# Moving the operand arena and the tile of block rests by 64 bytes in a hybrid two-block kernel

## The chip, the cores and the metric

The kernel runs on one core of a Trainium2 chip. The metric is the device time of one execution in microseconds, taken as the median of several executions. One execution was also recorded by the hardware profiler, and all rows shown here come from that record.

## The reference

The program computes two stacks of two layers each over a sequence of 512 tokens with 1024 features, all in float32. The first stack has in each layer a SwiGLU feed-forward, a mixer made of four parts (top-k sparse attention, gated linear attention, a causal convolution, and low-rank attention with rotary positions), and a second feed-forward. The second stack has a dilated-attention layer with a state-space part, then a layer with a gated linear recurrence, each followed by a feed-forward. Cut to what carries nearly all of the work:

```python
def rmsnorm(x, g):
    y = x32 * lax.rsqrt(jnp.mean(x32 * x32, axis=-1, keepdims=True) + EPS)
    return (y * g.astype(jnp.float32)).astype(x.dtype)

def swiglu(x, w_gate, w_up, w_down):            # [512,1024] x [1024,2816], twice; [512,2816] x [2816,1024]
    return (jax.nn.silu(x @ w_gate) * (x @ w_up)) @ w_down

def hybrid_layer(x, ...):                       # two of these
    x = x + 0.5 * swiglu(rmsnorm(x, ffn1_norm), ffn1_gate, ffn1_up, ffn1_down)
    z = rmsnorm(x, mix_norm) @ w_in
    ...                                         # four mixers on parts of z
    x = x + y @ w_out
    x = x + 0.5 * swiglu(rmsnorm(x, ffn2_norm), ffn2_gate, ffn2_up, ffn2_down)
    return x

def second_block(x, ...):                       # two layers
    mix = even_mixer(hn, ...) or odd_mixer(hn, ...)
    x = x + rms_norm(mix, norm_mix_post[layer])
    ff = swiglu_2(rms_norm(x, norm_ffn_pre[layer]), ffn_w_gate[layer], ffn_w_up[layer], ffn_w_down[layer])
    x = x + rms_norm(ff, norm_ffn_post[layer])
```

## The kernel before

Activations lie transposed: features on the 128 partitions, tokens along a row. A large product is made of matmuls with a stationary operand of 128x128 weights, which a weight load puts into the array, and a moving operand of 128 partitions by 512 or 256 tokens, which then streams through it. The next matmul's weight load runs while the present matmul streams, so TensorE reads two places of SBUF at once: the weights of the next matmul and the tokens of the present one.

Each float32 product is computed from split operands. A value is rounded to the type fp32r (the "hi" part) and the rest is kept beside it (the "lo" part). ScalarE writes the hi parts, VectorE the rests, and TensorE adds three products for each pair of tiles: weights hi by tokens hi, weights lo by tokens hi, weights hi by tokens lo. In `split_product` these are the lines L969, L970 and L971, always with 512 tokens. The tiles are `w_hi` (in `scratch`) and `w_lo` (in `wring`) for the weights, and for the tokens `f_hi`/`f_lo` (input of the six feed-forwards), `g_hi`/`g_lo` (their hidden values) and `z_hi` (input of the first stack's mixer projections), all in `arena`; `xn_hi` (input of the output projections and of the odd layer's projection) in `att_diag`; and `xn_lo` (the rests that go with `xn_hi` and `z_hi`) in `xn`.

The middle part of each of the six feed-forwards (`pe_ffn7`) computes its gate and up products in halves, by a scheme of seven block products instead of eight. Seven blocks j = 0 to 6 of weights, 128 partitions by 512 values each, are sums or differences of raw weight blocks. Each block takes 12 matmuls of 256 tokens: four pieces k, each with L1080 (block hi by `t_hi`), L1082 (block rest by `t_hi`) and L1083 (block hi by `t_lo`). The block rests lie in `p_lo_tile`, which shares its place with the raw sums `p_raw` in `att_diag`. `t_lo` lies in `arena`; `t_hi` lies in `xn` for blocks 0 to 3 (`t_hi_early`) and in `arena` for blocks 4 to 6 (`t_hi_late`). One group of seven blocks is one "kind" (gate or up) of one pair of hidden tiles. There are 9 pairs of 2 kinds in each of 6 feed-forwards, so 108 groups.

```python
            nc.tensor.matmul(ps, w_hi[:, slot, t, 0:M], hi, start=start, stop=False)
            nc.tensor.matmul(ps, w_lo[:, slot, t, 0:M], hi, start=False, stop=False)
            return nc.tensor.matmul(ps, w_hi[:, slot, t, 0:M], lo, start=False, stop=stop)
...
                            nc.tensor.matmul(ps, hi[:, k, :], t_hi(j)[:, k, :], start=(not again and k == 0), stop=False,
                                             skip_group_check=again)
                            nc.tensor.matmul(ps, lo[:, k, :], t_hi(j)[:, k, :], start=False, stop=False, skip_group_check=again)
                            mm = nc.tensor.matmul(ps, hi[:, k, :], t_lo[:, j, k, :], start=False, stop=(k == KH - 1),
                                                  skip_group_check=again)
```

The order of the work is written out by hand for each engine, with semaphores between them. The addresses within a partition are given by the order of allocation. `sb_aligned` puts a gap ahead of a tile so that it begins at a multiple of 512 bytes. The tiles `x`, `xn`, `wring`, `scratch`, `bias`, `arena` and `att_diag` all begin so. Every piece inside them is 512, 1024 or 2048 bytes long, with one exception: in `p_lo_tile` and `p_raw` the blocks are 2048 + 64 bytes apart (`BLK + GAP`, GAP being 16 words), so block j begins 64 x j bytes behind a multiple of 512.

Of the kernel before, what the change touches and what calls it, by code (L numbers as in the profile page):

```python
# [9 lines left out]
F32 = mybir.dt.float32  # L10
# [6 lines left out]
P = 128  # L17
SEQ = 512
TB = SEQ // P
# [11 lines left out]
B_HEADS, B_KEY, B_VAL, B_CHUNK, B_RANK = 4, 32, 64, 64, 16  # L31
# [194 lines left out]
HALF = SEQ // 2  # L226
KH = KD // 2
BLK = KH * P
GAP = 16
SCALED, FIRST_S3 = (1, 2, 5, 6), (3, 4)  # L230
SCALED_SUMS = 5 + GROUPS - 1
SUMS = KD + 4 + 3 * GROUPS
# [118 lines left out]
def program(nc, I, out):  # L351
    ctx = ExitStack()
    with ctx:
        at = {}

        def sb(name, shape, dt=F32):
            at[name] = -(-nc.sbuf_base // 32) * 32
            return ctx.enter_context(nc.sbuf_tensor(name, shape, dt))

        def over(name, shape, base, skip=0):  # L360

            return nc.alloc_sbuf_tensor_at(name, shape, F32R, offset=at[base] + skip)
# [4 lines left out]

        ALIGN = 512

        def sb_aligned(name, shape):  # L370
            gap = -(-(-nc.sbuf_base // 32) * 32) % ALIGN
            if gap:
                ctx.enter_context(nc.sbuf_tensor(f"gap_before_{name}", [P, gap // 4], F32))
            return sb(name, shape)

        x = sb_aligned("x", [P, KD, SEQ])
        xn = sb_aligned("xn", [P, KD, SEQ])
        y = xn
        wring = sb_aligned("wring", [P, 2, KD, 256])
        scratch = sb_aligned("scratch", [P, 11, SEQ])  # L380
        bias = sb_aligned("bias", [P, A_HEADS, SEQ])
        arena = sb_aligned("arena", [P, 46, SEQ])
        att_diag = sb_aligned("att_diag", [P, TB, B_HEADS, P])
        sb("block_gaps", [P, 8 * GAP])
        xn_more = sb("xn_more", [P, 2, SEQ])
        hpad = sb("hpad", [P, 2, TAPS - 1 + SEQ])
        b_mn, b_la = xn_more[:, 0, :], xn_more[:, 1, :]
# [29 lines left out]
        t_lo = over("t_lo", [P, 7, KH, HALF], "arena", 22 * SEQ * 4)  # L417
        t_hi_early = over("t_hi_early", [P, 4, KH, HALF], "xn")
        t_hi_late = over("t_hi_late", [P, 3, KH, HALF], "arena", 36 * SEQ * 4)
        p_lo_tile = over("p_lo_tile", [P, 8, BLK + GAP], "att_diag")[:, :, 0:BLK]  # L420
        p_raw = nc.alloc_sbuf_tensor_at("p_raw", [P, 8, BLK + GAP], F32, offset=at["att_diag"])[:, :, 0:BLK]
        g_lo = over("g_lo", [P, NF, SEQ], "arena")
        g_hi = over("g_hi", [P, NF, SEQ], "arena", 22 * SEQ * 4)
        gup = sb("gup", [B_RANK, P])
# [2963 lines left out]
```

## Time and profile before

| what | value |
|---|---|
| median of the runs | 3308.72 us (3306.56 to 3310.53, 3 runs) |
| the profiled execution, its own time | 3307.32 us |
| its span, first to last instruction | 3305.2 us |
| TensorE matmuls busy | 3196.7 us (97%), 18272 matmuls |
| weight loads busy | 2682.5 us (81%), beside the matmuls |
| VectorE busy | 2249.8 us (68%) |
| ScalarE busy | 1536.8 us (46%) |
| mean granted clock of TensorE | 0.989 |

The profiled execution took 2.1 us more than its span, and 1.4 us less than the median of the runs. A matmul's busy time in the profile includes its way through the array and overlaps with that of the next matmul, so what a matmul costs in a stream is the step from its start to the next one's start, and not its mean duration.

### The profile page before, as it was taken

What the parts mean: (1) busy time and instruction counts of PE and PEld (TensorE: products, weight loads), DVE (VectorE), ACT (ScalarE), POOL (GpSimd) and SP (SyncE); (2) the same over time, 40 slices, a digit from 0 to 9 for tenths busy, and PEclk for the clock granted to TensorE, in tenths of its full rate; (3) what the DMA queues carried; (4) which work ended last, traced back from release to release, by engine and by line L of the source; (5) the groups of instructions that cost most, each with busy time, mean ns of one, the idle gap of its engine ahead of it and who ended that gap; (6) DMA issues with size and microseconds to landing.
All of it is one profiled execution on the core that took longest, in us unless ns stands there. A gap on an engine that the chain in (4) does not pass through costs nothing.

```text
span 3305.2 us, 51513 instructions
## 1 busy us (share of the span) xinstructions
PE 3196.7 (97%) x18272; PEld 2682.5 (81%) x18272; DVE 2249.8 (68%) x3675; ACT 1536.8 (46%) x2795; POOL 241.7 (7%) x153
## 2 busy tenths in 40 slices
PE   7999999999999999999899999999899999999998
PEld 5998775779988899876578998565689986779986
DVE  5884489649854986388938873844398736679853
ACT  4553345445543554344535553213355524555543
POOL 0000002100000000000200000401000003110000
PEclk9999999899999999999999999999999999999999
DMA  4332331023323333332013332341133323223332
GB/s 140 107 102 100 85 83 53 1 81 100 113 96 95 100 104 97 100 83 78 1 52 100 104 101 90 97 95 37 52 90 102 102 96 95 72 78 106 102 102 76
DMA packets 420154, 286.41 MB, mean 87 GB/s; under 512 B 57416, under 2 KB 395180, under 8 KB 419884
## 3 DMA queue, kind: packets, MB, share of 16 engines
q1 hardware_dynamic: 419200, 283.62, 28.9%
q8 instruction: 77, 1.26, 0.2%
q10 hardware_dynamic: 828, 1.13, 0.1%
q14 instruction: 49, 0.40, 0.0%
HBM read 280.24 MB, written 4.47 MB: 86 GB/s over the span
## 4 chain that ended last, share of the span: by engine, by line
PE 79%; DVE 15%; ACT 3%; issue 3%; DMA 0%; POOL 0%; ACTq 0%; DVEq 0%; SPq 0%; POOLq 0%
PE bank L969 12%; PE bank L971 12%; PE bank L970 12%; PE bank L1080 10%; PE bank L1082 10%; PE bank L1083 10%; DVE t_lo L2388 1%; PE bank L964 1%; PE bank L1340 1%; PE bank L1339 1%; PE bank L1358 1%; DVE p_lo_tile L2361 1%; DVE w_lo L2347 1%; DVE arena L2419 1%; PE bank L1454 1%
## 5 line engine op out<-in xcount | busy, mean ns | idle before, releaser
L1083 PE MATMUL bank<-t_lo,w_hi 128*128 128x256 f32 x3024 | 851.3, 282 | 0.0
L2347 DVE TENSOR_TENSOR w_lo<-wring,w_hi 128x1024 fp32r<-128x1024 f32 x262 | 331.9, 1269 | 576.9 <-ACT w_hi L1707 576.5
L1707 ACT ACTIVATE w_hi<-wring 128x1024 fp32r<-128x1024 f32 x274 | 288.4, 1059 | 652.6 <-DMA wring<-in_ffn_down 278.5
L1083 PEld LDWEIGHTS bank<-t_lo,w_hi 128*128 128x128 f32 x3024 | 571.3, 189 | 0.0
L1082 PE MATMUL bank<-t_hi_early,p_lo_tile 128*128 128x256 f32 x1728 | 486.7, 282 | 0.0
L1080 PE MATMUL bank<-t_hi_early,w_hi 128*128 128x256 f32 x1728 | 485.6, 281 | 0.0
L971 PE MATMUL bank<-g_lo,w_hi 128*128 (+1 forms) x1056 | 410.9, 389 | 0.0
L970 PE MATMUL bank<-g_hi,w_lo 128*128 (+1 forms) x1056 | 410.8, 389 | 0.0
L969 PE MATMUL bank<-g_hi,w_hi 128*128 (+1 forms) x1056 | 410.8, 389 | 0.0
L1080 PE MATMUL bank<-t_hi_late,w_hi 128*128 128x256 f32 x1296 | 366.2, 283 | 9.8 <-ACT scratch L1795 8.9
L1082 PE MATMUL bank<-t_hi_late,p_lo_tile 128*128 128x256 f32 x1296 | 365.6, 282 | 0.0
L1719 ACT ACTIVATE w_hi<-p_raw 128x512 fp32r<-128x512 f32 x432 | 267.4, 631 | 199.4 <-DVE p_raw L2380 121.6
L2361 DVE TENSOR_TENSOR p_lo_tile<-p_raw,w_hi 128x512 fp32r<-128x512 f32 x432 | 287.9, 687 | 66.6 <-ACT w_hi L1719 56.7
L1082 PEld LDWEIGHTS bank<-t_hi_early,p_lo_tile 128*128 128x128 f32 x1728 | 328.2, 190 | 0.2
L1080 PEld LDWEIGHTS bank<-t_hi_early,w_hi 128*128 128x128 f32 x1728 | 326.9, 189 | 0.2
L1795 ACT ACTIVATE scratch<-bank 128x256 f32<-128x256 f32 x432 | 165.8, 384 | 274.8 <-PE bank L1083 267.6
L971 PE MATMUL bank<-xn_lo,w_hi 128*128 128x512 f32 (+1 forms) x680 | 266.9, 393 | 0.0
L2361 DVE TENSOR_TENSOR p_lo_tile<-wring,w_hi 128x512 fp32r<-128x512 f32 x324 | 222.7, 687 | 59.9 <-ACT w_hi L1719 56.8
L1080 PEld LDWEIGHTS bank<-t_hi_late,w_hi 128*128 128x128 f32 x1296 | 245.0, 189 | 12.0 <-issue 11.9
L1082 PEld LDWEIGHTS bank<-t_hi_late,p_lo_tile 128*128 128x128 f32 x1296 | 246.8, 190 | 0.0
L971 PEld LDWEIGHTS bank<-g_lo,w_hi 128*128 128x128 f32 x1056 | 198.2, 188 | 41.1
L970 PEld LDWEIGHTS bank<-g_hi,w_lo 128*128 128x128 f32 x1056 | 198.2, 188 | 41.1
(439 smaller groups left out, 5776.0 us busy)
## 6 DMA issues: line engine op xcount, KB each, us to landing
wring<-in_ffn_gate SPq DMA_DIRECT2D x88, 512.0 KB, 3.8
wring<-in_ffn_up SPq DMA_DIRECT2D x88, 512.0 KB, 3.9
wring<-in_ffn_down SPq DMA_DIRECT2D x88, 512.0 KB, 3.5
wring<-in_ffn_w_gate SPq DMA_DIRECT2D x44, 512.0 KB, 3.8
wring<-in_ffn_w_up SPq DMA_DIRECT2D x44, 512.0 KB, 3.8
wring<-in_ffn_w_down SPq DMA_DIRECT2D x44, 512.0 KB, 3.5
wring<-in_w_in SPq DMA_DIRECT2D x34, 512.0 KB, 3.6
wring<-in_w_out SPq DMA_DIRECT2D x16, 512.0 KB, 3.4
```

The costliest lines, as they stand in the source:

```text
L964: mm = nc.tensor.matmul(pb[MEAN_BANK][:, :], C("mean1024"), T(SQ + 2 * j), start=(j == 0), stop=(j == 3))
L969: nc.tensor.matmul(ps, w_hi[:, slot, t, 0:M], hi, start=start, stop=False)
L970: nc.tensor.matmul(ps, w_lo[:, slot, t, 0:M], hi, start=False, stop=False)
L971: return nc.tensor.matmul(ps, w_hi[:, slot, t, 0:M], lo, start=False, stop=stop)
L1080: nc.tensor.matmul(ps, hi[:, k, :], t_hi(j)[:, k, :], start=(not again and k == 0), stop=False, skip_group_check=again)
L1082: nc.tensor.matmul(ps, lo[:, k, :], t_hi(j)[:, k, :], start=False, stop=False, skip_group_check=again)
L1083: mm = nc.tensor.matmul(ps, hi[:, k, :], t_lo[:, j, k, :], start=False, stop=(k == KH - 1), skip_group_check=again)
L1707: nc.scalar.activation(w_hi[:, slot, :, :].rearrange("p k c -> p (k c)"), wunit[:, slot, :], ACT.Copy).then_inc(u_hi.h, 1)
L1719: nc.scalar.activation(p_hi_tile(st, j).rearrange("p k c -> p (k c)"), src, ACT.Copy).then_inc(u_hi.h, 1)
L1795: nc.scalar.activation(dst, src, ACT.Copy).then_inc(p_copied.h, 1)
L2347: nc.vector.tensor_tensor(w_lo[:, slot, :, :].rearrange("p k c -> p (k c)"), wunit[:, slot, :], w_hi[:, slot, :, :].rearrange("p k c -> p ...
L2361: tt(p_lo_tile[:, j, :], src, p_hi_tile(st, j).rearrange("p k c -> p (k c)").bitcast(F32), ALU.subtract).then_inc(u_lo.h, 1)
```

## The change

The tile `arena` and, behind it, `att_diag` begin 64 bytes behind a multiple of 512. The gaps between the blocks of `p_lo_tile` and `p_raw` are gone, so every block begins 64 bytes behind such a multiple. `x`, `xn`, `wring` (`w_lo`), `scratch` (`w_hi`) and `bias` keep their places. The small tiles behind `att_diag` (`xn_more`, `hpad`, the constants and columns) lie 448 bytes lower than before.

```diff
-GAP = 16
...
-        def sb_aligned(name, shape):
-            gap = -(-(-nc.sbuf_base // 32) * 32) % ALIGN
+        def sb_aligned(name, shape, past=0):
+            gap = (past - (-(-nc.sbuf_base // 32) * 32)) % ALIGN
             if gap:
                 ctx.enter_context(nc.sbuf_tensor(f"gap_before_{name}", [P, gap // 4], F32))
             return sb(name, shape)
...
-        arena = sb_aligned("arena", [P, 46, SEQ])
-        att_diag = sb_aligned("att_diag", [P, TB, B_HEADS, P])
-        sb("block_gaps", [P, 8 * GAP])
+        arena = sb_aligned("arena", [P, 46, SEQ], 64)
+        att_diag = sb_aligned("att_diag", [P, TB, B_HEADS, P], 64)
...
-        p_lo_tile = over("p_lo_tile", [P, 8, BLK + GAP], "att_diag")[:, :, 0:BLK]
-        p_raw = nc.alloc_sbuf_tensor_at("p_raw", [P, 8, BLK + GAP], F32, offset=at["att_diag"])[:, :, 0:BLK]
+        p_lo_tile = over("p_lo_tile", [P, 8, BLK], "att_diag")
+        p_raw = nc.alloc_sbuf_tensor_at("p_raw", [P, 8, BLK], F32, offset=at["att_diag"])
```

No instruction is added, removed or moved on any engine, and no wait changes; only addresses differ. In bytes behind a multiple of 512, the tiles that TensorE reads in its split products lie so:

| tile | role | before | after |
|---|---|---|---|
| `w_hi`, `w_lo` | weights | 0 | 0 |
| `p_lo_tile`, block j | weights | 64 x j | 64 |
| `g_hi`, `g_lo`, `f_hi`, `f_lo`, `z_hi`, `xn_hi` | tokens | 0 | 64 |
| `t_lo`, `t_hi_late` | tokens | 0 | 64 |
| `t_hi_early`, `xn_lo` | tokens | 0 | 0 |

## Rows read from the trace of the kernel before

**Rows 1.** The page: span, and busy time with share of each engine.

```profile
span 3305.2 us, 51513 instructions
...
PE 3196.7 (97%) x18272; PEld 2682.5 (81%) x18272; DVE 2249.8 (68%) x3675; ACT 1536.8 (46%) x2795; POOL 241.7 (7%) x153
```

**Rows 2.** The page: the chain that ended last, share of the span by engine.

```profile
PE 79%; DVE 15%; ACT 3%; issue 3%; DMA 0%; POOL 0%; ACTq 0%; DVEq 0%; SPq 0%; POOLq 0%
```

**Rows 3.** Groups by line and shape; count, busy us, mean ns, idle time before.

```profile
L1083 PE MATMUL bank<-t_lo,w_hi 128*128 128x256 f32 x3024 | 851.3, 282 | 0.0
L1083 PEld LDWEIGHTS bank<-t_lo,w_hi 128*128 128x128 f32 x3024 | 571.3, 189 | 0.0
...
L969 PEld LDWEIGHTS bank<-g_hi,w_hi 128*128 128x128 f32 x1056 | 198.2, 188 | 41.0
...
L970 PE MATMUL bank<-f_hi,w_lo 128*128 128x512 f32 x384 | 150.6, 392 | 0.0
...
L970 PE MATMUL bank<-xn_hi,w_lo 128*128 128x512 f32 x376 | 147.3, 392 | 0.0
...
L970 PE MATMUL bank<-z_hi,w_lo 128*128 128x512 f32 x288 | 113.7, 395 | 0.0
```

**Rows 4.** Timeline, PE: the first matmul of blocks 0 to 6, and the next 0.

```profile
112.83 0.28 PE L1080 MATMUL bank<-t_hi_early,w_hi 128*128 128x256 f32 x1
...
114.27 0.28 PE L1080 MATMUL bank<-t_hi_early,w_hi 128*128 128x256 f32 x1
...
115.68 0.28 PE L1080 MATMUL bank<-t_hi_early,w_hi 128*128 128x256 f32 x1
...
117.11 0.28 PE L1080 MATMUL bank<-t_hi_early,w_hi 128*128 128x256 f32 x1
...
118.52 0.28 PE L1080 MATMUL bank<-t_hi_late,w_hi 128*128 128x256 f32 x1
...
119.95 0.28 PE L1080 MATMUL bank<-t_hi_late,w_hi 128*128 128x256 f32 x1
...
121.36 0.28 PE L1080 MATMUL bank<-t_hi_late,w_hi 128*128 128x256 f32 x1
...
122.80 0.28 PE L1080 MATMUL bank<-t_hi_early,w_hi 128*128 128x256 f32 x1
```

**Rows 5.** Timeline, PE: matmuls 0, 9 and 18 of a down product (512 tokens).

```profile
262.33 0.39 PE L969 MATMUL bank<-g_hi,w_hi 128*128 128x512 f32 x1
...
264.40 0.39 PE L969 MATMUL bank<-g_hi,w_hi 128*128 128x512 f32 x1
...
266.44 0.39 PE L969 MATMUL bank<-g_hi,w_hi 128*128 128x512 f32 x1
```

**Rows 6.** Timeline, PE: two matmuls of a later down product, 39 matmuls apart.

```profile
1000.18 0.39 PE L969 MATMUL bank<-g_hi,w_hi 128*128 x1
...
1009.02 0.39 PE L969 MATMUL bank<-g_hi,w_hi 128*128 x1
```

**Rows 7.** The chain in order of time: plain float32 products, 512 and 256 wide.

```profile
2182.25 6.87 PE bank L1460 x16
...
2204.84 6.91 PE bank L1454 x32
```

**Rows 8.** Groups of DVE: rests of blocks 1, 2, 4, 5 and of 0, 3, 6.

```profile
L2361 DVE TENSOR_TENSOR p_lo_tile<-p_raw,w_hi 128x512 fp32r<-128x512 f32 x432 | 287.9, 687 | 66.6 <-ACT w_hi L1719 56.7
...
L2361 DVE TENSOR_TENSOR p_lo_tile<-wring,w_hi 128x512 fp32r<-128x512 f32 x324 | 222.7, 687 | 59.9 <-ACT w_hi L1719 56.8
```

**Rows 9.** Windows: a block section and the stage behind it, busy by engine.

```profile
80.76:262.33 181.57, 179.94 (x1513) 179.57 (x1512) 157.64 (x281) 107.91 (x226) 0.00 (x0) 1.00 0.36 107
262.33:382.04 119.71, 119.71 (x530) 99.13 (x529) 46.35 (x55) 37.71 (x49) 4.29 (x4) 1.00 0.30 92
```

**Rows 10.** DMA issues by line: transfers, KB each, median us to landing.

```profile
out_x<-arena SPq DMA_DIRECT2D x8, 256.0 KB, 2.0
```

## The prediction

> **What bounds the kernel now.** I read the page first. Matmuls are busy 97% of the span, and weight loads 81% beside them [rows 1]. The chain that ended last has PE for 79% of the span and DVE for 15% [rows 2]. In a block section PE is busy 179.9 of 181.6 us and DVE 157.6; in the down product behind it PE is busy all of the 119.7 us and DVE 46.4 [rows 9]. So in these stages the time is set by how closely TensorE's matmuls follow each other. The granted clock there is 1.00 [rows 9], the 2.4 GHz level, so nothing is to be had from the clock.
>
> Then I read steps from start to start. A down product's matmul with 512 tokens takes 8.84 us / 39 = 226.7 ns per step [rows 6]. The plain float32 products give a measure for a stream that is not squeezed: 6.87/16 = 429.4 ns for 512 columns and 6.91/32 = 215.9 ns for 256 [rows 7], so 0.834 ns for a column and 2.4 ns beside the columns. If a split product's column costs half of that, 512 of them cost 213.5, and with the 2.4 the step would be 215.9 ns. It is 226.7. So 10.8 ns of each step are unexplained by streaming. The next weight load runs during this step and reads SBUF too. That the two reads disturb each other is my reading, and the block products speak for it: there, instructions and shapes are alike from block to block, and only the address of the block's rests changes.
>
> The steps over twelve matmuls of blocks 0 to 6 are 1.44, 1.41, 1.43, 1.41, 1.43, 1.41 and 1.44 us, together 9.97 [rows 4]; the same pattern comes back in the other groups. Blocks 1, 3 and 5, whose rests lie 64, 192 and 320 bytes behind a multiple of 512, are 1.5 to 2% quicker than block 0, where everything lies at 0. So the distance between what is loaded and what streams, in steps of 64 bytes, does set TensorE's pace, by some 2 ns in 118. VectorE shows nothing of the kind: a rest takes 687 ns in blocks 1, 2, 4, 5 and 687 in blocks 0, 3, 6 [rows 8].
>
> **The change, part by part.** No instruction and no wait changes, so there is no term for added or removed work.
>
> Part A, block products. There are 108 groups, 84 matmuls each, 9072 together (3024 for each of three lines [rows 3]). After the change the rests lie at 64 in each block. In blocks 4 to 6 both kinds of tokens lie at 64 too, and the hi weights at 0. Measured from the tokens that stream, the hi weights are at -64 and the rests at 0. In block 1 before, they were at 0 and +64. The difference between rests and hi weights is the same 64, with everything slid by a constant, so I take block 1's pace, 1.41: these blocks go from 1.43 + 1.41 + 1.44 = 4.28 to 4.23, or 0.05 x 108 = 5.4 us less. In blocks 0 to 3 the hi tokens stay at 0 and only `t_lo` goes to 64, which is a pattern that no block had. From 5.69 they would go to 5.64 at best, again 5.4 us; I take half, 2.7 us. Part A: -8.1 us. The bounds: all seven at 1.41 gives 9.87, -10.8 us; all at 1.44 gives 10.08, +11.9 us.
>
> Part B, products with 512 tokens. Their weights stay at 0, and the tokens go to 64 for `g` (1056 x 3), `f` (384 x 3), `xn_hi` (376 x 2) and `z_hi` (288 x 2) [rows 3], 5648 matmuls. All of them stood at distance 0 before, so the trace has no row for the new distance; I bound it. From below: the step can't be shorter than the 215.9 ns of an undisturbed stream, -10.8 x 5648 = -61 us, far off since no block came near such a gain. A third of it, 3.6 ns, is -20 us. From above: right behind a block section the first nine steps of a down product take 2.07/9 = 230.0 ns and the next nine 2.04/9 = 226.7 [rows 5]. The operands are alike, so two paces are possible at one and the same distance, and the stream settles at the lower. If the new distance doesn't let it settle, each step costs 3.3 ns more, +18.8 us. In between, the six blocks with a distance average 1.422 us against 1.44, 1.5 ns less a matmul, with one load of three at a distance. But 512 columns have settled at one pace wherever I looked, and a constant slide of all tokens may simply be taken up by when the reads start. I take 0.6 ns of those 1.5: -3.4 us.
>
> Part C, the rest. Plain products leave no room for a gain, as they stand at 2.4 ns beside their columns [rows 7]. VectorE and ScalarE are taken as unchanged [rows 8]; what covers a small loss there is PE, busy throughout [rows 9]. Transfers to and from `arena` start 64 bytes off. The last one, out of `arena`, takes 2.0 us to land [rows 10]; a tenth of it would be 0.2 us, and I take 0.
>
> The Trainium skill, DMA: Bandwidth & Descriptors, section How a descriptor splits into AXI transactions, has a transaction start at a 256-byte boundary, so that a descriptor 64 bytes behind one costs additional beats. By that the last transfer would be longer, not shorter; no row here shows an offset transfer.
>
> Sum: -8.1 - 3.4 = -11.5 us on the profiled execution's 3307.3 is 3295.8. The median of the runs is 1.4 above that execution, so 3297.2 us, 0.35% less. A faster TensorE would be held by DVE only if a block section fell under DVE's 157.6 us plus its waits; it falls by 1.4.
>
> **The rivals.**
>
> *Slower, the 512-wide stream no longer settles.* Place: the 5648 matmuls of part B. For it: rows 5's two paces, and that 0/0 is the distance at which it settles now; `xn_hi` and `xn_lo` and the early blocks also mix two distances after the change. Against it: in the blocks distance 0 is the slowest, not the quickest. Price +18.8 us; with part A at nothing 3327.5 us, with both upper bounds 3339. It decides from 8.1/5648 = 1.4 ns a matmul on, where it has eaten part A.
>
> *No change that can be measured.* The slide is taken up entirely in the 512-wide products (part B 0), and of part A the late blocks' 5.4 us at most stay: 3303 to 3309 us. For it: a uniform slide changes no distance from one matmul's stream to the next. Against it: late and early blocks both had slower members that leave.
>
> The Trainium skill, TensorE: Matmul & The Clock Gate, section Step-by-step: what each phase is for, gives TensorE two independent read ports, one for each operand, and the Trainium skill, SBUF — State Buffer, section Who interferes with whom, says that PE never waits on anyone. Read strictly, addresses would then do nothing and the time would stay at 3308.7; the blocks' 1.41 against 1.44 [rows 4] disagree, and that is why I give this rival no more than its share. The Trainium skill, TensorE: Matmul & The Clock Gate, section Back-to-back issue gap, has 518 cycles for 512 columns, 215.8 ns at 2.4 GHz, which rows 7 meet and rows 6 do not.
>
> *A large gain.* The distance frees a third of the 10.8 ns: -20 - 8 = -28 us, 3280 us. For it: the quick blocks have only one load of three at a distance, and in part B all three have one. Against it: block 3 and block 1 are equally quick at different distances, so it looks like a plateau.
>
> **How the numbers follow.** About 0.2% (6.6 us) is what a measurement of this kernel can tell from no change. Forecast (3285 to 3302): 0.35. Large gain (below 3285): 0.11. No change (3302 to 3315): 0.24. Slower: 0.30. So faster 0.46, same 0.24, slower 0.30. The range leaves out half of the large gain's reach and the top of the slower case, less than 2 in 10 together: 3266 to 3335. The forecast's own range is 3285 to 3302.
>
> **What would show it.** In the changed profile the twelve-matmul steps of all seven blocks should be near 1.41, with blocks 4 to 6 alike. A down product's 39 steps should take 8.80 to 8.84 us. If they take over 8.9, the slower rival holds; if near 8.7, the large gain. If blocks 0 to 3 show 1.43 or more, the half I took for them was wrong. Counts, order and the durations of DVE and ACT should be as before; if a rest on DVE is no longer 687 ns, part C is wrong. The prediction falls as a whole if the pace depends on something that moves with the blocks' number other than the rests' address, since block number and address go together in the rows I have.

## The result: 0.30% slower, where 0.35% faster was forecast

The changed kernel's median is 3316.2 us (3315.1 to 3320.0, 8 runs), against 3308.7 us (3306.0 to 3310.5, 8 runs) for the kernel before on the same chip. The ratio is 1.0030, with a 95% interval of 1.0021 to 1.0039. The profiled execution took 3315.1 us and its span is 3313.1, 7.9 us more than before.

The page of the changed kernel, span, busy time and chain, answers to [rows 1, 2]:

```profile
span 3313.1 us, 51513 instructions
...
PE 3206.7 (97%) x18272; PEld 2673.9 (81%) x18272; DVE 2251.6 (68%) x3675; ACT 1536.5 (46%) x2795; POOL 241.6 (7%) x153
...
PE 84%; DVE 10%; ACT 2%; issue 2%; DMA 0%; POOL 0%; ACTq 0%; DVEq 0%; SPq 0%; POOLq 0%
```

Counts are as before. PE's busy time rose by 10.0 us and its share of the chain from 79% to 84%. VectorE rose by 1.8 us and ScalarE by nothing. So the time went to TensorE. The groups by line and shape, which answer to [rows 3] (L1083, L970 are now L1081, L968), say to which matmuls:

```profile
L1081 PE MATMUL bank<-t_lo,w_hi 128*128 128x256 f32 x3024 | 853.8, 282 | 0.0
...
L968 PE MATMUL bank<-f_hi,w_lo 128*128 128x512 f32 x384 | 151.3, 394 | 0.0
L968 PE MATMUL bank<-xn_hi,w_lo 128*128 128x512 f32 x376 | 149.7, 398 | 0.0
...
L968 PE MATMUL bank<-z_hi,w_lo 128*128 128x512 f32 x288 | 115.4, 401 | 0.0
```

The 256-wide ones stay at 282 ns. The 512-wide ones grew by 2, 6 and 6 ns (they were 392, 392 and 395). Their steps from start to start are the better measure. First the blocks, in the timeline of PE, first matmuls of blocks 0 to 6 and of the next block 0, as in [rows 4]:

```profile
113.16 0.28 PE L1078 MATMUL bank<-t_hi_early,w_hi 128*128 128x256 f32 x1
...
114.57 0.28 PE L1078 MATMUL bank<-t_hi_early,w_hi 128*128 128x256 f32 x1
...
115.98 0.28 PE L1078 MATMUL bank<-t_hi_early,w_hi 128*128 128x256 f32 x1
...
117.39 0.28 PE L1078 MATMUL bank<-t_hi_early,w_hi 128*128 128x256 f32 x1
...
118.81 0.28 PE L1078 MATMUL bank<-t_hi_late,w_hi 128*128 128x256 f32 x1
...
120.22 0.28 PE L1078 MATMUL bank<-t_hi_late,w_hi 128*128 128x256 f32 x1
...
121.63 0.28 PE L1078 MATMUL bank<-t_hi_late,w_hi 128*128 128x256 f32 x1
...
123.04 0.28 PE L1078 MATMUL bank<-t_hi_early,w_hi 128*128 128x256 f32 x1
```

Every block takes 1.41 us, and a group of seven 9.88 instead of 9.97. This half of the forecast came true. Next the 512-wide products: the timeline of PE at matmuls 0, 9 and 18 of the first down product [rows 5], at two matmuls of a later one, 39 apart [rows 6], and at two of an output projection, 39 apart:

```profile
261.46 0.39 PE L967 MATMUL bank<-g_hi,w_hi 128*128 128x512 f32 x1
...
263.53 0.39 PE L967 MATMUL bank<-g_hi,w_hi 128*128 128x512 f32 x1
...
265.59 0.39 PE L967 MATMUL bank<-g_hi,w_hi 128*128 128x512 f32 x1
...
670.38 0.40 PE L967 MATMUL bank<-xn_hi,w_hi 128*128 128x512 f32 x1
...
679.48 0.40 PE L967 MATMUL bank<-xn_hi,w_hi 128*128 128x512 f32 x1
...
999.53 0.39 PE L967 MATMUL bank<-g_hi,w_hi 128*128 x1
...
1008.46 0.39 PE L967 MATMUL bank<-g_hi,w_hi 128*128 x1
```

The first nine steps take 2.07/9 = 230.0 ns as before, but the next nine 2.06/9 = 228.9 instead of 226.7, and it stays there: 8.93/39 = 229.0. In the projection, where `xn_hi` lies at 64 and `xn_lo` at 0, it is 9.10/39 = 233.3 ns. Over the steps between two matmuls of `split_product` that run without a break (about 6,260 of 6,384 in each trace, all under 300 ns) the mean is 230.1 ns against 226.9, together 20.4 us more.

What remains as it was: VectorE's rests (first two rows, 688 and 689 ns, [rows 8]), the plain float32 products in the chain of waits (6.87 us for 16 and 6.91 for 32, [rows 7]) and the last transfer (2.0 us, [rows 10]):

```profile
L2359 DVE TENSOR_TENSOR p_lo_tile<-p_raw,w_hi 128x512 fp32r<-128x512 f32 x432 | 288.4, 688 | 62.0 <-ACT w_hi L1717 52.2
...
L2359 DVE TENSOR_TENSOR p_lo_tile<-wring,w_hi 128x512 fp32r<-128x512 f32 x324 | 223.3, 689 | 57.0 <-ACT w_hi L1717 56.0
```

```profile
2198.06 6.87 PE bank L1458 x16
2209.36 6.91 PE bank L1452 x32
```

```profile
out_x<-arena SPq DMA_DIRECT2D x8, 256.0 KB, 2.0
```

Windows of the changed kernel, all engines, cut at the same matmuls as [rows 9] for the first two; the third is the first layer's mixer, the fourth the output projection behind it:

```profile
81.61:261.46 179.85, 178.32 (x1514) 178.08 (x1512) 157.17 (x279) 107.89 (x226) 0.00 (x0) 1.00 0.36 108
261.46:382.32 120.86, 120.86 (x530) 99.27 (x529) 46.45 (x55) 37.75 (x49) 4.30 (x4) 1.00 0.29 91
538.34:665.41 127.07, 112.98 (x586) 74.30 (x584) 96.81 (x241) 69.24 (x171) 33.67 (x26) 0.96 0.02 5
665.41:710.29 44.88, 44.88 (x196) 36.11 (x194) 12.74 (x15) 11.25 (x15) 0.00 (x0) 1.00 0.26 83
```

The same two later stages in the kernel before:

```profile
535.17:666.76 131.59, 117.62 (x585) 77.77 (x584) 97.22 (x241) 69.20 (x171) 33.55 (x26) 0.94 0.02 5
666.76:710.41 43.65, 43.65 (x195) 36.14 (x194) 12.60 (x15) 11.16 (x14) 0.00 (x0) 1.00 0.28 85
```

Cut in this way from end to end, the account is:

| stages | before | after | difference |
|---|---|---|---|
| six block sections (181.57 to 179.85 in the first) | 1089.5 | 1080.0 | -9.5 us |
| stages with 512-wide split products (119.71 to 120.86, 43.65 to 44.88, ...) | 1652.7 | 1673.3 | +20.6 us |
| the rest, -4.5 of it in the mixer above (131.59 to 127.07) | 563.0 | 559.8 | -3.2 us |
| span | 3305.2 | 3313.1 | +7.9 us |

The mixer's 4.5 us is read as the clock's and not the change's. The granted clock of that stage is 0.94 in one record and 0.96 in the other, and the second layer's stage of the same shape took 126.3 us in the kernel before. An experiment below (`blocks128`) has 0.94 and 131.5 us in the second layer instead.

### The profile page after: what moved, and what is told of

Its sections match the earlier page's. It is cut to its first block, busy times and chain, and to the rows that moved or that the text cites. A ratio compares the mean times of both kernels' runs of the same rounds, so it can differ in the third digit from the quotient of the medians.

```text
span 3313.1 us, 51513 instructions
## 1 busy us (share of the span) xinstructions
PE 3206.7 (97%) x18272; PEld 2673.9 (81%) x18272; DVE 2251.6 (68%) x3675; ACT 1536.5 (46%) x2795; POOL 241.6 (7%) x153
## 4 chain that ended last, share of the span: by engine, by line
PE 84%; DVE 10%; ACT 2%; issue 2%; DMA 0%; POOL 0%; ACTq 0%; DVEq 0%; SPq 0%; POOLq 0%
PE bank L967 13%; PE bank L968 13%; PE bank L969 13%; PE bank L1081 10%; PE bank L1078 10%; PE bank L1080 10%; PE bank L1458 3%; PE bank L962 1%; PE bank L1338 1%; PE bank L1337 1%; DVE t_lo L2386 1%; PE bank L1356 1%; DVE p_lo_tile L2359 1%; DVE arena L2417 1%; PE bank L1452 1%
## 5 line engine op out<-in xcount | busy, mean ns | idle before, releaser
L1081 PE MATMUL bank<-t_lo,w_hi 128*128 128x256 f32 x3024 | 853.8, 282 | 0.0
L1081 PEld LDWEIGHTS bank<-t_lo,w_hi 128*128 128x128 f32 x3024 | 568.8, 188 | 0.0
L968 PE MATMUL bank<-g_hi,w_lo 128*128 (+1 forms) x1056 | 416.5, 394 | 0.0
L967 PEld LDWEIGHTS bank<-g_hi,w_hi 128*128 128x128 f32 x1056 | 198.4, 188 | 46.0
```

## The experiments

My theory after the result: with 512 tokens any distance between the two places that TensorE reads costs, although with 256 tokens one gains, and the projections pay extra for mixing two distances. The rivals: it is the address itself, or `arena`'s neighbours, or something that only the two parts together do. In the table "group" is the time of 84 block matmuls (seven blocks) in settled groups, and "512 step" the mean over the about 6,260 unbroken steps of the 512-wide products, both from each kernel's trace. The experiments ran on four chips. Compare the ratios, each of which is taken against the kernel before on the same chip (medians of 3307.4 to 3308.1 us).

| kernel | weights hi, lo / tokens / block rests | median us (runs) | ratio, interval | group us | 512 step ns |
|---|---|---|---|---|---|
| before | 0, 0 / 0 / 64 x j | 3308.7 (8) | 1 | 9.97 | 226.9 |
| the change | 0, 0 / 64, some 0 / 64 | 3316.2 (8) | 1.0030, 1.0021 to 1.0039 | 9.89 | 230.1 |
| `rests_only` | 0, 0 / 0 / 64 | 3298.6 (12) | 0.9977, 0.9969 to 0.9986 | 9.89 | 226.9 |
| `all_slid` | 64, 64 / 64 / 128 | 3299.8 (9) | 0.9977, 0.9968 to 0.9987 | 9.89 | 226.9 |
| `tokens64` | 0, 0 / 64 / 64 | 3310.1 (10) | 1.0009, 1.0000 to 1.0018 | 9.89 | 229.0 |
| `tokens128` | 0, 0 / 128 / 192 | 3321.5 (5) | 1.0039, 1.0026 to 1.0052 | 9.80, 9.71 | 232.7 |
| `tokens192` | 0, 0 / 192 / 128 | 3335.5 (4) | 1.0089, 1.0073 to 1.0104 | 9.93 | 233.3 |
| `wlo64` | 0, 64 / 0 / 64 | 3321.7 (4) | 1.0045, 1.0030 to 1.0061 | 9.89 | 231.2 |
| `wlo128` | 0, 128 / 0 / 64 | 3322.1 (4) | 1.0047, 1.0030 to 1.0064 | 9.89 | 231.2 |
| `wlo192` | 0, 192 / 0 / 64 | 3320.1 (6) | 1.0039, 1.0026 to 1.0051 | 9.89 | 231.1 |
| `gaps_kept` | 0, 0 / 64, some 0 / 64 + 64 x j | 3313.7 (9) | 1.0023, 1.0013 to 1.0033 | 9.84 | 230.0 |
| `blocks128` | 0, 0 / blocks 128, others 0 / 64 | 3285.4 (7) | 0.9930, 0.9916 to 0.9943 | 9.80, 10.08 | 226.9 |
| `blocks128_r0` | 0, 0 / blocks 128, others 0 / 0 | 3308.8 (10) | 1.0004, 0.9994 to 1.0013 | 9.97 | 226.9 |
| `blocks128_r192` | 0, 0 / blocks 128, others 0 / 192 | 3301.6 (11) | 0.9986, 0.9977 to 0.9995 | 9.89, 10.08, 9.97 | 226.9 |

**`rests_only`**: one part alone, the rests of all blocks at 64 and every other tile as before.

```diff
-        p_lo_tile = over("p_lo_tile", [P, 8, BLK + GAP], "att_diag")[:, :, 0:BLK]
+        p_lo_tile = over("p_lo_tile", [P, 8, BLK], "att_diag", 64)     # p_raw likewise
```

> Only the block rests move: every block of p_lo_tile begins 64 bytes behind a multiple of 512, and arena, att_diag and all tokens stay at 0. Theory (pace is set by the distance between what is loaded and what streams): all seven blocks take 1.41 us, a block section 180 us in place of 181.6, six of them 9 us less; the 512-wide products keep 226.7 ns, since nothing of theirs moved; 3300 us, ratio 0.997 to 0.998. Rival (the blocks owe their new pace to the tokens that moved, or to all tiles of arena): the blocks keep 1.43 and 1.41 in turn and the time stays within 2 us of 3308.7.

The timeline of PE: block 0 of two groups in a row, and the two matmuls of [rows 6].

```profile
113.81 0.28 PE L1080 MATMUL bank<-t_hi_early,w_hi 128*128 128x256 f32 x1
...
123.70 0.28 PE L1080 MATMUL bank<-t_hi_early,w_hi 128*128 128x256 f32 x1
...
993.53 0.39 PE L969 MATMUL bank<-g_hi,w_hi 128*128 x1
...
1002.37 0.39 PE L969 MATMUL bank<-g_hi,w_hi 128*128 x1
```

The group takes 9.89 us as in the change, and 39 steps 8.84 us as before. It is faster than before by 0.23%, and than the change by 0.53%. So the block rests alone bring 7.2 of the block sections' 9.5 us (1082.3 us for all six; the settled groups are as quick as in the change to 0.01 us, and it is mainly the first group that differs, 10.27 against 9.89 us in the first section). The loss belongs wholly to the slide of the token tiles. With the rests at one address all seven blocks take 1.413 us, so it was the address, and not the block's number, that made the pattern of [rows 4].

**`all_slid`**: as `rests_only`, with every tile slid by 64 (and the rests at 128).

```diff
-        x = sb_aligned("x", [P, KD, SEQ])
+        x = sb_aligned("x", [P, KD, SEQ], 64)      # and xn, wring, scratch, bias, arena, att_diag
```

> All large tiles, weights and tokens alike, begin 64 bytes behind a multiple of 512, and the rests another 64 behind that. Every distance is that of rests_only, every address is 64 higher. Theory (only distances count): same time and same paces as rests_only, 3300 us, 512-wide products at 226.7 ns. Rival (tokens of the arena at 64 are slow as such, by their address): 512-wide products at 229 to 234 ns as in the changed kernel, 3320 us.

It came out as `rests_only` in every column. An address 64 bytes behind a multiple of 512 costs nothing; the distance does.

**`tokens64`**: the change without its mixture; `t_hi_early` and `xn_lo` go to 64 as well.

```diff
+        xn = sb_aligned("xn", [P, KD, SEQ], 64)    # now behind bias
         arena = sb_aligned("arena", [P, 46, SEQ], 64)
         att_diag = sb_aligned("att_diag", [P, TB, B_HEADS, P], 64)
```

> All tokens at 64, xn too (it is allocated ahead of arena for that); weights at 0, rests at 64. Against the changed kernel xn_lo and t_hi_early move, so that no product mixes two distances. Theory A (both the distance and the mixing cost): g and f stay at 229.1 ns, z falls from 231 and xn_hi from 233.5 to 229.1 as well; about 6 us less than the changed kernel, 3310 us. Theory B (the distance alone costs, mixing nothing): no difference to the changed kernel, 3316 us. Theory C (mixing alone costs): all products back at 226.7, 3298 us.

The timeline of PE in the same output projection, 39 matmuls apart, as shown above for the change:

```profile
665.09 0.39 PE L967 MATMUL bank<-xn_hi,w_hi 128*128 128x512 f32 x1
...
674.02 0.39 PE L967 MATMUL bank<-xn_hi,w_hi 128*128 128x512 f32 x1
```

The median met the forecast of 3310 us, and 8.93/39 is 229.0 ns, against 233.3 in the change. Of the 20.4 us that the change's 512-wide steps cost, `tokens64` keeps 13.5 (14.84 over 226.67 ns a step against 1.36 in the kernel before), so 13.5 are for the distance and 6.9 for the mixture of distances. Theory A held.

**`tokens128`** and **`tokens192`**: the same with larger distances, in the three lines above 128 or 192, and the rests at 192 or 128.

> All tokens at 128, weights at 0, rests 64 behind a multiple of 256. Maps the 512-wide pace over the distance. Theory (at distance 0 the stream settles, at others it need not): between 226.7 and 234 ns, time 3298 to 3330 us. If 128 is as good as 0 the blocks' pattern says why: 1.43 at a rest distance of 128 against 1.41 at 64. Rival (distance 0 is the worst for wide streams as it is for the blocks): under 226 ns, below 3295 us; the changed kernel already speaks against that for 64.

> As tokens128, with all split tokens (arena, att_diag, xn) at 192 and the block rests at 128, so tokens less weights is +192 (or -64 modulo 256) for both hi and lo weights of the 512-wide products. Theory A (the pace has a period of 128 bytes, and the sign of 64 does not matter): as tokens64, 512-wide steps of 229.1 ns, blocks 1.413 us, 3305 to 3314. Theory B (the sign matters, or the loss grows with the distance): steps of 232 ns or more, 3320 to 3335.

Down steps of [rows 6] in `tokens192`, then in `tokens128`, where a group of blocks from the third section stands behind them (timeline of PE):

```profile
1003.83 0.39 PE L967 MATMUL bank<-g_hi,w_hi 128*128 x1
...
1012.93 0.40 PE L967 MATMUL bank<-g_hi,w_hi 128*128 x1
```

```profile
998.93 0.40 PE L967 MATMUL bank<-g_hi,w_hi 128*128 x1
...
1008.04 0.39 PE L967 MATMUL bank<-g_hi,w_hi 128*128 x1
...
1138.37 0.28 PE L1078 MATMUL bank<-t_hi_early,w_hi 128*128 128x256 f32 x1
...
1148.08 0.28 PE L1078 MATMUL bank<-t_hi_early,w_hi 128*128 128x256 f32 x1
```

At 192 the step is 9.10/39 = 233.3 ns and the kernel is the slowest of all, so theory A fell: 64 and -64 (which 192 is, if 256 bytes close the circle) are not alike. Theory B held, its range to 3335 passed by 0.5 us. At 128 the step is 9.11/39 = 233.6, inside the wide range given, and the rival (under 226 ns) fell. But there the blocks run at 9.80 us a group, and in two sections at 9.71, faster than anything seen before. That is also the first kernel in which sections with the same addresses keep to different paces. Quickest for the 256-wide stream, among the slowest for the 512-wide one: the two can't be argued from each other.

**`wlo64`**, **`wlo128`**, **`wlo192`**: as `rests_only`, with only `w_lo` moved, one weight load of three. This gives the 512-wide stream what block 1 had in the kernel before.

```diff
-        wring = sb_aligned("wring", [P, 2, KD, 256])
+        wring = sb_aligned("wring", [P, 2, KD, 256], 64)      # 128, 192 in the other two
```

> As rests_only, but w_lo (one weight load of three in every 512-wide product) begins 64 bytes behind a multiple of 512; tokens and w_hi stay at 0. This is for the 512-wide stream what block 1 was for the 256-wide one. Theory A (any distance keeps the 512-wide stream from its settled 226.7 ns): steps between 227.5 and 229.5 ns, +5 to +18 us on rests_only, 3303 to 3316. Theory B (rests 64 bytes away help here as in the blocks, 1.5 ns or more per matmul): steps of 225.5 ns or less, 3286 to 3294.

> As wlo64, with w_lo 128 bytes behind a multiple of 512 while w_hi and the tokens of the 512-wide products stay at 0. wlo64 measured 231.1 ns per step and 3321.7 us. Theory A (the 512-wide stream settles at 226.7 ns only where all it reads lies at the same place modulo 256): 229 ns or more here too, 3310 us or more; the size is open, up to 234 ns and 3335. Theory B (only odd multiples of 64 disturb, 128 is as good as 0 or better): 226.7 ns or less, 3299 or less.

> As wlo64, with w_lo at 192, that is 64 ahead of the others modulo 256 instead of 64 behind. Theory A (a step depends on the way from one address to the next around 256 bytes, so the three steps of a triple only change places and the mean stays): 231.1 ns, 3319 to 3324. Theory B (the sign matters, as 229 against 233 ns between tokens64 and tokens192): a mean off 231.1 by 1 ns or more, so under 3315 or over 3326.

The timeline of PE in `wlo64`: a triple of a down product, the first matmul of the next triple, and the matmul 39 steps behind the first:

```profile
999.26 0.39 PE L969 MATMUL bank<-g_hi,w_hi 128*128 x1
999.49 0.40 PE L970 MATMUL bank<-g_hi,w_lo 128*128 x1
999.73 0.39 PE L971 MATMUL bank<-g_lo,w_hi 128*128 x1
999.96 0.39 PE L969 MATMUL bank<-g_hi,w_hi 128*128 x1
...
1008.28 0.39 PE L969 MATMUL bank<-g_hi,w_hi 128*128 x1
```

All three measure 231.1 ns per step (9.02/39). In the down products of `wlo64` the step behind each `w_lo` matmul is the long one, 235.8 ns on average, and the other two are 229.2 and 228.3. In `wlo128` the three are 234.1, 232.5 and 226.7, the longest again behind `w_lo`. In `wlo192` the longest, 233.3, stands behind `g_lo`, and the others are 230.9 and 229.2. Theory A held for `wlo128`. For `wlo192` it gave the right mean and time, but its reason fell: the three steps did not change places, they have other sizes that add up to the same 693 ns. Why the sum stays is not shown. In `wlo64` theory B fell, and A's sign held with a size (4.3 ns a step, median 3321.7) above its range. The arrangement that makes a block 1.5 to 2% quicker makes a 512-wide product 1.9% slower.

**`gaps_kept`**: the change with the 64-byte gaps between blocks put back.

```diff
+        sb("block_gaps", [P, 8 * GAP])
-        p_lo_tile = over("p_lo_tile", [P, 8, BLK], "att_diag")
+        p_lo_tile = over("p_lo_tile", [P, 8, BLK + GAP], "att_diag")[:, :, 0:BLK]      # p_raw likewise
```

> The change with one part undone: arena and att_diag at 64, but the 64-byte gaps between blocks kept, so the rests of block j lie at 64 + 64 x j. The 512-wide steps should be those of the change, 230.2 ns on average, whatever the blocks do. Theory A (what counts is the rests' distance to the hi weights, which lie at 0): blocks 0, 2, 4, 6 at 1.41 us and 1, 3, 5 at 1.43. Theory B (what counts is the rests' distance to the tokens they are multiplied with, at 0 in blocks 0 to 3 and at 64 in 4 to 6): blocks 0, 2 and 5 at 1.41, and 1, 3, 4, 6 at 1.43. Either way 108 x 0.06 to 0.08 = 6 to 9 us more than the change, median 3321 to 3326.

The timeline of PE: first matmuls of blocks 4, 5, 6 and the next 0.

```profile
118.08 0.28 PE L1080 MATMUL bank<-t_hi_late,w_hi 128*128 128x256 f32 x1
...
119.49 0.28 PE L1080 MATMUL bank<-t_hi_late,w_hi 128*128 128x256 f32 x1
...
120.86 0.28 PE L1080 MATMUL bank<-t_hi_late,w_hi 128*128 128x256 f32 x1
...
122.27 0.28 PE L1080 MATMUL bank<-t_hi_early,w_hi 128*128 128x256 f32 x1
```

The 512-wide step was 230.0 ns, close to the 230.2 expected. For the blocks both theories fell: none ran at 1.43, the medians were 1.411, 1.416, 1.411, 1.413, 1.409, 1.365 and 1.415, and block 5 took only 1.37. Its median is 2.5 us under the change's, which the intervals don't tell apart, and not 6 to 9 us above. In block 1 the rests lay 128 from the hi weights and from `t_hi`, as in block 2 before, and only `t_lo` lay elsewhere; it took 1.416 us against 1.432. So no rule in one distance describes the blocks.

**`blocks128`**, **`blocks128_r0`**, **`blocks128_r192`**: an attempt to have both, 512-wide products at distance 0 and blocks at the distance of `tokens128`, with the rests at 64, 0 and 192.

```diff
-        f_hi = over("f_hi", [P, KD, SEQ], "arena", 14 * SEQ * 4)
-        t_lo = over("t_lo", [P, 7, KH, HALF], "arena", 22 * SEQ * 4)
-        t_hi_early = over("t_hi_early", [P, 4, KH, HALF], "xn")
+        f_hi = over("f_hi", [P, KD, SEQ], "arena", 14 * SEQ * 4 - 256)     # f_lo likewise
+        t_lo = over("t_lo", [P, 7, KH, HALF], "arena", 22 * SEQ * 4 - 128) # t_raw, t_hi_late likewise
+        t_hi_early = over("t_hi_early", [P, 4, KH, HALF], "xn", 128)       # a gap behind xn
+        p_lo_tile = over("p_lo_tile", [P, 8, BLK], "att_diag", 64)         # 0, 192 in the others
```

> Block rests at 64, as in rests_only; the blocks' tokens (t_lo, t_hi) stand 128 bytes from their hi weights (modulo 256), which is the arrangement that gave 1.400 us for a block; the tokens of the 512-wide products stay at distance 0, but f_hi and f_lo are slid by 256 bytes. Theory A (distances alone set the pace, each stage for itself): every block 1.400 us, a block section 177 to 178.5 us against 180.3 in rests_only, the 512-wide steps 226.7 ns for g, z, xn and f alike, median about 3284 us (3298.6 less some 15). Theory B (the 1.400 us came from another tile that moved along in tokens128): blocks stay at 1.413, median 3298 to 3301. If 256 bytes are not the same as 0 for the 512-wide stream, f alone goes to 229 ns or more: 3 to 8 us more than theory A.

> As blocks128, with the block rests at 0, where the hi weights stand; so both weight loads of a block are 128 bytes from the tokens. Theory A (the rests must stand an odd multiple of 64 from the tokens, and 128 counts as 0 for them): blocks slower than 1.413, about 1.42 to 1.43 us, median 3300 to 3308. Theory B (only the distance of the hi weights to the tokens made the step from 1.413 to 1.400): blocks near 1.40 to 1.41, median 3284 to 3297.

> As blocks128, with the block rests at 192 instead of 64, so they stand 64 behind the blocks' tokens (128) instead of 64 ahead of them, as in tokens128; one small tile moves into the gap behind xn to make room. In the profile of blocks128 two block sections ran at 1.400 us a block (178.8 us) and four at 1.440 (183.3 us), all with the same addresses, and its runs lay between 3281 and 3312. Theory A (at a distance of 128 the rests' side decides whether the slow rhythm exists; tokens128 never showed it): all sections at 1.387 to 1.400 us a block, 176.6 to 178.8 us, 512-wide steps 226.7 ns, median 3278 to 3284, runs within 8 us of each other. Theory B (both rhythms exist at 128 whatever the rests do, and how a section is entered decides): some sections at 1.440 again, runs between 3280 and 3312.

Windows of `blocks128`, PE alone: the first block section, the second, and the second layer's mixer.

```profile
81.29:260.18 178.89, 176.96 (x1514) 1.00 0.36 109
751.02:934.42 183.40, 181.64 (x1514) 1.00 0.35 106
1557.46:1688.99 131.53, 117.41 (x586) 0.94 0.02 5
```

The first section runs at 1.400 us a block throughout and the second at 1.440, in one execution, with the same instructions, addresses and granted clock. Two of its six sections had the quick rhythm and four the slow one. Its runs were 3281.0, 3281.4, 3281.7, 3285.4, 3286.0, 3307.3 and 3312.0 us (the last is the profiled one). Theory A's 3284 was met by the median but not by the trace. With all six sections quick this record would be 18 us shorter, near 3294, and the runs of 3281 are shorter still. No trace of them was kept, so what their sections did is not shown. With the rests at 192 three rhythms appeared (9.89, 10.08 and four times 9.97 us a group), so theory B held there. With the rests at 0 there was one, 9.97, and no gain: theory A held, its median 0.8 us above the range. The products of `f_hi` and `f_lo`, 256 bytes off, ran at 227.0 ns against 226.9 in the kernel before, so 256 bytes count as 0 there.

So `blocks128` is the fastest version by its median, but not dependable from run to run. `rests_only` is the best of the steadier ones, 0.23% under the kernel before (eleven of its twelve runs lie within 4.5 us).

## Why the prediction was wrong

**Where the time is set: right.** PE sets it in these stages, and addresses alone move it. The Trainium skill, SBUF — State Buffer, section Who interferes with whom, has PE never wait on anyone. These traces can't say whom it waits for, but its step goes from 226.7 to 233.6 ns by nothing but where operands lie. The measurement decides against reading that sentence as one on speed.

The 215.9 ns of "an undisturbed stream" is another matter. It rests on the assumption that a split product's column costs half a plain one's, and in no run is the mean step of the 512-wide split products under 226.7. [rows 7] meet it only by that halving: their 512-wide products take 429.4 ns, and 215.9 is what a 256-wide one takes. So the 10.8 ns that the large gain drew on were not shown to be there.

**Part A: right.** Forecast -8.1 us, measured -9.5 over the six block sections. The late blocks went from 4.28 to 4.23 us as forecast. The early ones went from 5.69 to 5.65, where I had taken half of the way to 5.64. The rule behind it, that a block goes by the distance between its rests and its hi weights, is weaker than the number: it holds for the arrangement of the change and fell in `gaps_kept`. About 1.8 of the 9.5 us lie in the first groups of the sections, which I had not looked at.

**Part B: wrong, and this is the step that failed**: "I take 0.6 ns of those 1.5: -3.4 us." It measured +20.6 us over the stages, +3.3 ns a step in place of -0.6. I had carried the sign over from the 256-wide blocks to the 512-wide products, and `wlo64` shows that the same arrangement has opposite signs in the two kinds of product. My argument against the slower rival, that "in the blocks distance 0 is the slowest", was this same transfer. My second argument, that "a constant slide of all tokens may simply be taken up by when the reads start", fell with `tokens64`, which is such a slide and costs 2.2 ns a step.

The upper bound of 18.8 us was also too low. It counted 5648 matmuls and left out the 664 of `xn_lo`, which kept their addresses but stand between slid ones: they went to about 232 ns. And it had one distance in mind, while mixing two in one product cost 6.9 us of the 20.4. Its 3.3 ns met the measured 3.3 by luck, since it was read from the entry of a stream and not from a distance.

**Part C: right.** VectorE 688 and 689 ns against 687, plain products unchanged. The last transfer now starts 64 bytes off and still lands in 2.0 us, so the longer one that the prediction weighed was not seen.

**The slower rival** named the place and nearly the price: part A's -9.5 and its own 18.8 would give 3318. Its mechanism was off. The stream does settle, within nine steps, but at another rhythm. Rows 5's first 230.0 ns are an entry that both kernels share. It was said to decide from 1.4 ns a matmul on, and 3.3 came. The signs I had set, "over 8.9, the slower rival holds", read 8.93.

**How much of a step reaches the end**: against `rests_only` (span 3295.8 us) the 512-wide steps cost 20.4 us more in the change, 26.7 in `wlo64` and 40.1 in `tokens192`, and the spans are longer by 17.3, 24.1 and 36.5. Of the 3 to 4 us between, 2.3, 2.7 and 1.3 are block sections that are shorter than in `rests_only`. So TensorE's pace reaches the end nearly one for one.

**Still open**: why distances act so. What is shown is that the pace stays when all addresses slide alike (`all_slid`), that 256 bytes are as good as 0 for the 512-wide products (`f_hi` in `blocks128`), and that 512-wide steps at distance 0 are the quickest of the eight arrangements tried. Which access waits for which was not seen. For the blocks, and in `tokens128` for the 512-wide steps too, even the outcome isn't fixed by addresses; how a section is entered may pick the rhythm, which is argued and not shown.

## What to carry to other kernels

Where a stream of matmuls is the bound, weights and tokens that are split for fp32r are worth placing deliberately: the same 64 bytes gave 0.23% in one place and took 0.5% in another. Try the placement per shape of matmul and never carry a sign from one width to another. Move one tile at a time, since `rests_only`, one part of the change, held 7.2 of its 9.5 us of gain and none of its loss. And when one execution shows one stage at two paces, read the stage's steps in every section before calling a median a speed.

## What the runs showed of the hardware that was not expected

- A settled stream of fp32r matmuls repeats itself in short cycles. With all operands at the same place modulo 256 it has one step (226.7 ns). With the tokens of `g` at 64 it has three unequal ones, 229.2, 231.7 and 225.9 ns in the change (mean 228.9); in `gaps_kept`, where these tiles lie as in the change, the same three stand one matmul further on. In the first down product of `tokens192` two steps alternate, 231 and 236 ns, and in that of `tokens128` 229 and 237 or 238.
- The same code at the same addresses can keep to 1.400 or 1.440 us a block for a whole section of 180 us (`blocks128`), 2.8% apart, at a granted clock of 1.00. In `tokens128` it is 1.400 or 1.387, and there the down products behind the two quickest sections settle at 232.4 ns a step, those behind the other four at 233.3.
- Moving `w_lo` by 64, 128 or 192 bytes costs the same 4.4 ns a step (231.1 against 226.7), but divides the triple otherwise: its longest step is 235.8, 234.1 or 233.3 ns, and at 192 it stands behind another matmul.
- The mixer stages, with PE at 89% busy, ran at a mean granted clock of 0.94, 0.96 or 0.97 from record to record, which moves the span by 5 us with no change in the code, while this change moved it by 7.9.
